# First attention of a two-block network: the two heads of a feature tile go through TensorE as a pair

## The reference, cut to what matters

```python
s_c = einsum('bsghd,bngd->bsghn', qr, kc) * scale      # branch 0: 31 compressed keys
p_c = softmax(where(m_c, s_c, NEG)) * m_c
o_cmp = einsum('bsghn,bngd->bsghd', p_c, vc)
# branch 1: selected blocks. SEQ/64 = 8 blocks, the 16 best are taken: all of them, so causal attention
# branch 2: window of 512 over 512 positions: causal attention with its own keys and values
o = g[..., 0:1] * o_cmp + g[..., 1:2] * o_sel + g[..., 2:3] * o_win
```

```python
sv = einsum('gts,bnsgc->bntgc', w, v) + bs.T[None, None, :, :, None]
return u * sv.reshape(B, S, GM_WIDTH)
```

## Time and profile before

| | us |
|---|---|
| median of 3 runs | 3685.18 |
| lowest, highest | 3680.12, 3686.68 |
| the profiled execution | 3684.62 |
| its span, first to last instruction | 3682.8 |
| PE busy | 3581.1 (97%) |
| DVE busy | 2167.7 (59%) |
| ACT busy | 1324.0 (36%) |
| mean granted TensorE clock | 0.984 |

### The profile page before, as it was taken

How to read it: one execution, slowest core, us unless ns; L and a number is a source line. 1 busy time by engine, 2 the same in 40 slices (tenths; PEclk the granted TensorE clock), 3 DMA queues, 4 the chain that set the end, 5 groups by cost and what they waited for, 6 DMA issues and landing times.

```text
span 3682.8 us, 47040 instructions
## 1 busy us (share of the span) xinstructions
PE 3581.1 (97%) x18600; PEld 2939.7 (80%) x18600; DVE 2167.7 (59%) x3611; ACT 1324.0 (36%) x1941; POOL 292.9 (8%) x382
## 2 busy tenths in 40 slices
PE   6999999999999999999999999999999999999998
PEld 5888864889888988886588988889988888578887
DVE  6455544546555555564466776877776556655444
ACT  3222444224222422244432432345533236544222
POOL 1000112001000100011300101002100001210000
PEclk9999989999999999998999999999999999999999
DMA  6444210343444244421034434443544422002221
GB/s 240 176 155 156 99 62 3 127 148 139 176 155 171 104 172 162 153 95 51 20 116 142 158 140 155 155 150 131 183 167 153 149 73 75 20 35 103 94 101 47
DMA packets 85386, 452.03 MB, mean 123 GB/s; under 512 B 10320, under 2 KB 12816, under 8 KB 48304
## 3 DMA queue, kind: packets, MB, share of 16 engines
q1 hardware_dynamic: 83088, 439.35, 32.3%
q0 software_dynamic: 2080, 9.67, 0.8%
HBM read 446.88 MB, written 2.10 MB: 122 GB/s over the span
## 4 chain that ended last, share of the span: by engine, by line
PE 89%; DVE 5%; ACT 2%; issue 2%; DMA 1%; POOL 0%; DVEq 0%; SPq 0%; ACTq 0%; POOLq 0%
PE ps L621 21%; PE ps L620 21%; PE ps L619 21%; PE ps L1507 3%; PE ps L1543 2%; PE ps L3184 1%; DVE WL L537 1%; PE ps L996 1%; PE ps L998 1%; PE ps L997 1%; PE ps L1525 1%; ACT WH L526 1%; PE ps L2490 1%; PE ps L2491 1%; PE ps L1247 1%
## 5 line engine op out<-in xcount | busy, mean ns | idle before, releaser
L537 DVE TENSOR_TENSOR WL<-raw,WH 128x2048 fp32r<-128x2048 f32 (+2 forms) x308 | 674.7, 2197 | 397.6 <-ACT WH L526 394.4
L621 PE MATMUL ps<-nH,WL 128*128 128x512 f32 x2272 | 891.9, 393 | 0.0
L620 PE MATMUL ps<-nL,WH 128*128 128x512 f32 x2272 | 891.3, 392 | 0.0
L619 PE MATMUL ps<-nH,WH 128*128 128x512 f32 x2272 | 889.8, 392 | 1.3 <-DVE vf L1877 0.9
L526 ACT ACTIVATE WH<-raw 128x2048 fp32r<-128x2048 f32 (+2 forms) x308 | 560.0, 1824 | 608.4 <-PE ps L621 494.0
L619 PEld LDWEIGHTS ps<-nH,WH 128*128 128x128 f32 x2272 | 427.2, 188 | 98.7 <-issue 4.4
L620 PEld LDWEIGHTS ps<-nL,WH 128*128 128x128 f32 x2272 | 427.3, 188 | 94.8 <-issue 0.2
L621 PEld LDWEIGHTS ps<-nH,WL 128*128 128x128 f32 x2272 | 427.3, 188 | 90.5
L585 DVE SCALAR_TENSOR_TENSOR araw<-araw,cB 128x1024 f32<-128x1024 f32 x225 | 276.6, 1229 | 212.5 <-DMA araw<-in_ast 212.3
L619 PE MATMUL ps<-hH,WH 128*128 128x512 f32 x944 | 372.6, 395 | 6.6 <-DVE h L1214 5.7
L621 PE MATMUL ps<-hH,WL 128*128 128x512 f32 x944 | 372.5, 395 | 0.0
(11 more groups left out here) (423 smaller groups left out, 5984.6 us busy)
## 6 DMA issues: line engine op xcount, KB each, us to landing
raw<-in_wst SPq DMA_DIRECT2D x282, 1024.0 KB, 4.8
araw<-in_ast SPq DMA_DIRECT2D x225, 512.0 KB, 5.7
raw<-in_wst SPq DMA_DIRECT2D x18, 512.0 KB, 3.3
row<-in_ast SPq DMA_DIRECT2D x15, 512.0 KB, 15.0
cw<-in_cw POOLq DMA_DIRECT2D x4, 1024.0 KB, 5.9
h<-in_xT SPq DMA_DIRECT2D x1, 2048.0 KB, 8.3
raw<-in_wst SPq DMA_DIRECT2D x8, 256.0 KB, 2.6
out<-h SPq DMA_DIRECT2D x16, 128.0 KB, 1.8
```

The costliest lines, as they stand in the source:

```text
L537: dve.q.tensor_tensor(M.WL[k % NW][:, 0:n], M.raw[k % NR][:, 0:n], M.WH[k % NW][:, 0:n].bitcast(F32), ALU.subtract).then_inc(*v_wlo.up(k))
L619: pe.q.matmul(to, hi[:, i, cc], xh, start=i == 0, stop=False)
L620: pe.q.matmul(to, hi[:, i, cc], xl, start=False, stop=False)
L621: t = pe.q.matmul(to, lo[:, i, cc], xh, start=False, stop=i == nk - 1)
```

## The change

The unit of work on PE becomes a pair: the same branch and query tile of both heads of a feature tile (`PAIRS`, 36 of them). The scores of the two heads, which use different halves of the rows, are issued one behind the other, then both masks. The values of the two heads, which use different halves of the columns, are issued alternately, chunk by chunk. `NEAR` and `FAR` are now 2 and 3 pairs. Since both heads are in work at once, a second `PT` per branch is needed: it lies in the tiles `raw0` and `raw1`, so the two weight pieces that were loaded into them during the attention are loaded after its last dense values (`behind_attention`). ACT now copies all transposes of the first head, DVE all of the second. In the gated unit the loops over chunk and half are exchanged.

```diff
+def behind_attention(slots):
+    out = {}
+    for l in range(2):
+        k = [s[:2] + (s[4],) for s in slots].index(("mix_w_in", (l,), 1280))
+        for i in range(NR):
+            out[k + NW + i] = l
+    return out
...
-            M.PT = [sb(at, f"PT{i}", [128, 4, S]) for i in range(2)]
+            M.PT = [[sb(at, f"PT{i}", [128, 4, S]) for i in range(2)],
+                    [M.raw[i][:, :].rearrange("p (a b) -> p a b", a=4) for i in range(2)]]
...
-        NEAR, FAR = 4, 6
+        NEAR, FAR = 2, 3
...
+            for n in range(N1 + FAR):
+                if n < N1:
+                    scores1_pe(pe, g, n)
+                if NEAR <= n < N1 + NEAR:
+                    for u in pair_of(n - NEAR):
+                        turn1_pe(pe, g, u)
+                if n >= FAR:
+                    values1_pe(pe, g, n - FAR)
...
+            for hf in range(2):
+                half, K = halves[hf], (M.ko if hf == grp else M.ks)[br - 1]
+                pe.q.matmul(to[hf][:, 0:nk], M.q[half, ft, 128 * qt:128 * qt + 128], K[half, 0:nk], start=True, stop=False,
+                            skip_group_check=True)
+            for u, b in zip(pair_of(n), to):
+                pe.q.matmul(b[:, nk - 128:nk], M.idb[:, :], M.negm[:, :], start=False, stop=True,
+                            skip_group_check=True).then_inc(*mm.up(g, "s", u))
...
+                for x in range(4):
+                    for hf in range(2):
+                        t = pe.q.matmul(to[halves[hf], 128 * x:512], M.Vt[br - 1][:, x, cols],
+                                        M.PT[hf][br - 1][:, x, 128 * x:512], start=br == 1 and x == 0, stop=False,
+                                        skip_group_check=True)
+                        if x == 3:
+                            t.then_inc(*mm.up(g, "v", 2 * ft + hf, br))
...
-            if br and qt % 2:
+            if br:
...
+            for k in (now.split["dve"] - 2, now.split["dve"] - 1):
+                dve.wait_ge(*a_whi.to(k))
+                dve.wait_ge(*v_wlo.to(k))
+            for n in range(N1 + FAR):
+                for u in pair_of(n - 1) if 1 <= n <= N1 else ():
+                    inverse1_dve(dve, g, u)
+                for u in pair_of(n) if n < N1 else ():
+                    top1_dve(dve, g, u)
+                for u in pair_of(n - NEAR) if NEAR <= n < N1 + NEAR else ():
+                    turned1_dve(dve, g, u)
+                if n >= FAR:
+                    out1_dve(dve, g, 2 * (n - FAR) + 1)
...
-                for hf in range(2):
-                    for x in range(4):
-                        pe.wait_ge(*v_ln.to(g, x))
+                for x in range(4):
+                    pe.wait_ge(*v_ln.to(g, x))
+                    for hf in range(2):
...
+                if k in late:
+                    sp.wait_ge(*mm.to(f"mix{late[k]}", "v", 7, 2))
```

More of the change, by code:

```diff
@@ L1498, in score1_pe, with pair_of, scores1_pe @@
+        def pair_of(n):
+            return 2 * n, 2 * n + 1
+        def scores1_pe(pe, g, n):
+            ft, br, qt = PAIRS[n]
+            to = []
+            for u in pair_of(n):
+                b, free = take(g, "s", u)
+                pe.wait_ge(*free)
+                to.append(b)
+            halves, grp = (slice(0, 64), slice(64, 128)), ft // 2
             if br == 0:
                 for x in range(4):
-                    pe.q.matmul(b[:, 32 * x:32 * x + 32], M.q[half, hh // 2, 128 * x:128 * x + 128], M.kc[half, grp, :],
-                                start=x == 0, stop=False, skip_group_check=True)
@@ L1502, in score1_pe @@
-                pe.q.matmul(b[:, 0:128], M.idb[:, :], M.cneg[:, :], start=False, stop=True,
-                            skip_group_check=True).then_inc(*mm.up(g, "s", u))
+                    for b, half in zip(to, halves):
+                        pe.q.matmul(b[:, 32 * x:32 * x + 32], M.q[half, ft, 128 * x:128 * x + 128], M.kc[half, grp, :],
+                                    start=x == 0, stop=False, skip_group_check=True)
+                for u, b in zip(pair_of(n), to):
+                    pe.q.matmul(b[:, 0:128], M.idb[:, :], M.cneg[:, :], start=False, stop=True,
+                                skip_group_check=True).then_inc(*mm.up(g, "s", u))
@@ L1526, in turn1_pe, with values1_pe @@
             t.then_inc(*mm.up(g, "t", u))
[L1528 to L1532, removed]
-            if br == 0:
-                pe.wait_ge(*v_ev.to(g, "t", u))
-                pe.q.matmul(to[half, :], M.vc[:, 64 * grp:64 * grp + 64], lat.scr[hh % 2][0:32, :], start=False, stop=True,
-                            skip_group_check=True).then_inc(*mm.up(g, "v", hh, 0))
+        def values1_pe(pe, g, n):
+            ft, br, qt = PAIRS[n]
+            ua, ub = pair_of(n)
+            to, cols = banks[6 + ft % 2], slice(64 * (ft // 2), 64 * (ft // 2) + 64)
+            halves = (slice(0, 64), slice(64, 128))
+            if br == 0:
+                pe.wait_ge(*v_ev.to(g, "t", ua))
+                pe.wait_ge(*v_ev.to(g, "t", ub))
+                for hf in range(2):
+                    pe.q.matmul(to[halves[hf], :], M.vc[:, cols], lat.scr[hf][0:32, :], start=False, stop=True,
+                                skip_group_check=True).then_inc(*mm.up(g, "v", 2 * ft + hf, 0))
             elif qt == 3:
@@ L1539, in value1_pe @@
                     pe.wait_ge(*a_ev.to(g, "y", ft - 2))
-                pe.wait_ge(*v_ev.to(g, "t", u - 1))
-                pe.wait_ge(*a_ev.to(g, "t", u))
+                pe.wait_ge(*a_ev.to(g, "t", ua))
+                pe.wait_ge(*v_ev.to(g, "t", ub))
                 for x in range(4):
[L1543 to L1546, removed]
+                    for hf in range(2):
[4 more added lines that the diff above has]
+                            t.then_inc(*mm.up(g, "v", 2 * ft + hf, br))
         def copy_act(act, g, dst, src, wait):
@@ L1765, in out1_dve @@
             hh, br, qt = UNITS[u]
-            if br or hh % 2 == 0:
+            if br:
                 return
@@ L3458, in pool_program @@
             rest_pool(pool)
+        late = behind_attention(slots)
         def sp_program(sp):
```

52 lines of the change are left out of this document (21 added, 31 removed).

## The result

The changed kernel took 3600.27 us (median of 4 runs, 3596.82 to 3601.63), the kernel before 3682.84 us (4 runs, 3680.12 to 3686.68). The ratio is 0.9774, with a 95% interval from 0.9757 to 0.9791: faster by 82.6 us. The forecast was 3627 us, 57.4 less.

A forecast was written before the change was run, and what follows sets the result against it. PE was taken as the limit. Per layer, 105 us of tiles, 1.5 to the first exponential and 6.5 cold start gave 113 against 141.2; 56.4 in all plus 1.0 for gated units saved 57.4: 3627 us, range 3613 to 3642.

The forecast's parts named there:

- late loads: Weight pieces loaded after the attention's last dense values: hidden by ready slots; without that cover, 10 us a layer.
- DVE's wait for ACT at the output: Once per feature tile DVE waits for ACT's two copies, some 2 us, with the next maxima queued behind.
- the branch 0 pair: Branch 0 scores of both heads on PE: mere weight loads, priced at 1.9 us, twice 1.00 less a little.
- the cold start: Start of each attention: clock falls again until the first values, 17 us at half clock instead of 11, costing 6.5.
- the tile's sum: Attention time per feature tile: 26.3 us, from the ring's 20.9 plus additions where PE is last; 105 per layer.
- the ring: DVE and ACT loop of maximum, exponentials, reciprocal, next maximum: 20.9 us per feature tile, not hidden behind PE's equal sum.
- large transposes: Two attention steps per feature tile with large transposes on PE: 0.7 us added.
- the 0.10 on each score pair: Added to the 1.05 us of a 512-key score pair on PE, because the second head's weights load first.
- The first: Rival: the ring doesn't close and PE runs by its own sum in the attention: 3586 us, chance 0.13.
- The second: Rival: clock falls inside the attention once per feature tile, 3.5 us each, 28 back: 3655 us, chance 0.16.
- The third: Rival: one kind of half doesn't overlap; rows 34 us in all, 3661; columns 37, 3664; chance 0.13 together.
- The fourth: Rival: slower, as PE's waits in the ring keep the attention at half clock throughout: 3762 us, chance 0.05.

The follow-up runs named there:

- e2: Changed kernel with the value products of a pair issued head by head, four then four, instead of alternating: 3622.48 us.
- e5: Changed kernel with the gated unit's loops in the old order, half outside and chunk inside; attention unchanged: 3601.77 us in one run.
- e6: Changed kernel with the first head's mask between the two heads' scores in the first four score pairs of each layer only: 3609.64 us.
- e1: Changed kernel with the first head's mask between the two heads' scores in every pair, so row halves can't run together: 3685.35 us.
- e10: e1 plus two unneeded whole-array 128x128 products ahead of each pair's scores, which overwrite them: 3670.57 us.
- e8: Changed kernel with DVE making both maxima of a pair ahead of both reciprocals of the pair before: 3608.58 us.
- e3: Changed kernel with the edits of e1 and e2 together: 3733.82 us, 1.0137 of the kernel before.
- e4: Changed kernel with DVE taking the low part of the output one step later: 3587.65 us.
- e11: e4 plus, in the one step after branch 0, DVE's reciprocals behind the next pair's maxima: 3584.4 us.
- e7: Changed kernel with PE making the values of pair n-3 ahead of the transposes of pair n-2: 3626.58 us.
- e9: Changed kernel with the edits of e4, e7 and e8 together: 3617.43 us.

## Why the prediction was right and wrong

**Right: what bound the kernel and what the halves do.** PE was the limit, and the value pair came at 2.31 us where 2.30 was forecast. The rule of the Trainium skill ("TensorE: Matmul & The Clock Gate", Part 3, what overlaps and what doesn't) that was set aside for columns would have made it 4.60; these runs side with the earlier trace rows, and e2 puts the price of losing two thirds of the overlap at 22 us. The gated unit's loops gave 0.5 a layer, late loads cost nothing, and DVE's wait for ACT at the output was 1.96 us where 2 stood. DVE's maxima waited for PE as forecast, seldom but behind values: of the 14.5 us in 13 waits, 13.0 are seven waits of 1.8 to 1.9 us right behind value products. PE was busy for 20.8 us per feature tile (41.54 for two) where 20.9 stood, which is in part luck: the branch 0 pair took 0.9 less than its price, and busy time also counts the ends of the records ahead of each wait. One reading of the earlier trace rows was off: of the ten records of its second row eight start in it and two had started before, so the rate doubles and no more. The conclusion stands.

**Wrong: the cold start.** The step that failed is "what it does there is hardly changed, so I let it fall again", 6.5 us a layer. The term is too large by all or nearly all of itself. Layer 0's clock stayed up; the start had 3.4 us at half clock in layer 1 and 6.8 in e5's layer 1, where 17 were forecast, and even those 6.8 cost only 0.5 us, since PE waits in these steps anyway. The first pairs are where the change acts first, and e6, which takes it away for four pairs alone, brings back 13.7 and 10.2 us at half clock and 9.4 us of the time, in which the four pairs' longer scores are included. I had read the clock as something that the idle time ahead of it decides; e1, e6 and e10 show that with PE busy all along, the clock is low for half of the attention where score products fill one half of the rows at a time, and for far less where both halves run together or whole-array products are added.

**Wrong: the tile's sum, 26.3 against 24.2.** The step that failed is that PE's sum and the ring of maximum, exponential and reciprocal "don't hide each other", so that every step without values was priced at the ring's time. For the four steps that have neither values nor an output or branch 0 (384 and 512 keys of branch 1, 256 and 512 of branch 2) the ring makes 2.04 + 2.39 + 1.69 + 2.39 = 8.5 us (the middle sizes taken between the two that the forecast works out), and up to 0.7 for large transposes comes to it. They took 2.29 + 1.72 + 1.73 + 1.72 = 7.5, and PE's timeline shows no wait in them. That is 1.0 to 1.7 of the 2.1 us. The ring is still there, but it isn't what these steps wait for, and opening it everywhere (e8) won nothing. The step with branch 1's values took 3.61 instead of 4.05, partly because the 0.10 on each score pair wasn't there. Around branch 0 the forecast holds as a whole (3.85 + 0.2 + 5.4 against 2.32 + 1.52 + 5.54, 9.4 each), though the time sits a step later. The scores of the branch 0 pair, put at 1.9 us, took 1.01, since the weight loads of the two row halves also run side by side; little hung on it, because the ring was the longer there. The wait at the output, which the prediction had and priced, is real: a step of 3.71 where 1.34 + 2.2 stood.

**The balance.** 113.0 forecast less 100.1 measured is 12.9 us for layer 0: 6.5 for the cold start and 8.4 for the tiles (105 forecast less 4 x 24.16), less 1.6 for the one fall of the clock inside (25.7 us for that tile against 24.2) and 0.4 at the ends. Layer 1 gives 12.6, so the two attentions came out 25.5 us shorter than forecast, of the 26.7 by which the whole did.

**The rivals.** The first (3586) had the direction: PE found slack, but still waits 14 us a layer, and 3600 lies between the two. The second appeared behind one output in each layer of the profiled execution, and behind three of three in e5's layer 0, at 1.1 to 1.6 us a time instead of 3.5. The third did not happen, and e1 shows why it was priced much too low: 34 us for rows that don't overlap, when it is 85. The fourth expected PE's waits to keep the clock low. That isn't what a low clock came with here: in e3, the only version slower than before, 85 and 102 us pass at half clock while PE is busy for 162.21 of 163.03, with the halves apart. The Trainium skill ("TensorEngine Tiling (Array Packing)", PSUM Bottleneck) warns that emptying PSUM can become the limit under packing; here DVE is busy for 65.3 of 100.1 us, and the two waits that are left to PE stand behind its order, as e4 and, less surely, e11 show, and not behind its load.

**Open.** Why e7 and e8 have a fall of the clock in nearly every tile, and how their loss divides between that and the longer steps; the changed attention itself has had one to three falls in a layer. Why the clock stays low with the halves apart is not shown either, only that it does. The 15 and 30 us of e1 are an estimate from its steps at full clock.

## What to carry to other kernels

Two products that each use half of the array's rows or columns should be issued next to each other, with no whole-array product between them (e1), and in turns: two records of each head in a row still overlapped fully (the scores), eight in a row lost two thirds of the overlap (the values, e2). Look at the granted clock of a stretch with half-filled products even where the engine is busy throughout, since filling both halves can be worth more through the clock than through the overlap (e1, e10). Once TensorE is faster, read what stands ahead of its releaser in another engine's order: a low part that nobody is waiting for cost 12.6 us until it went one step later (e4), and took falls of the clock with it. Such a move must be measured alone: values ahead of transposes and maxima ahead of reciprocals looked as good and cost 26 and 8 us (e7, e8), and together with the good one gave its gain back (e9).

## What the runs showed of the hardware that was not expected

- TensorE can be busy for 23.80 of 23.80 us and run mostly at the lower of its two clock levels, 1.2 GHz instead of 2.4 (0.55 granted, e1), and adding useless whole-array products to it made the kernel 15 us faster (3670.57 against 3685.35, e10).
- Row halves overlap, the records with their weight loads: 16 records of 32 columns in 1.01 us (542.46 to 543.47), as long as 8 before.
- Column halves overlap fully if they alternate (2.31 us for the pair, 2.30 for one head). If not, TensorE begins the second half's products three records early (3.85 us for the pair): in e2 one starts at 571.50, ahead of the first head's at 571.72. The Trainium skill ("TensorE: Matmul & The Clock Gate", Part 3, what overlaps and what doesn't) has matmul starts strictly in order; this trace doesn't agree.
